# A streaming encoder layer on one core: one pass per tile with its own history length, and the modulation's products in four column groups

## The chip, the core and the metric

The kernel runs on one core of a Trainium2 chip. The metric is the device time of one execution in microseconds: 3823.52 as the median of three runs (3816.02 to 3826.64). The profile is of one further execution. Engines are named as the profile does: PE is TensorE (PEld its weight loads), DVE is VectorE, ACT is ScalarE, POOL is GpSimd, SP is SyncE, which issues most transfers.

## What is computed

One layer is applied to 64 new positions of a sample sequence (with 512 cached keys) and to a prompt of 1024 positions:

```
mod = silu(c) @ w_ada + b_ada            # c: (1024,), w_ada: (1024, 6144)
sh1, sc1, g1, sh2, sc2, g2 = split(mod, 6)
h   = rms_norm(x)*(1+sc1) + sh1
x   = x + g1 * (concat[SSD(h), FoX(h), ChunkMLP(h)] @ w_out)
x   = x + g2 * PEER(rms_norm(x)*(1+sc2) + sh2)
```

SSD is a chunked state-space scan, FoX is causal attention with a forget gate (4 heads of 64, blocks of 128 queries over all earlier keys), ChunkMLP mixes positions inside chunks of 128. PEER picks 128 experts for each position by product keys and sums their rows. All is float32. There are two vectors c, one of the prompt and one of the sample, so the modulation is a product of a 2 x 1024 matrix with w_ada.

## The kernel before

The program has two blocks; a barrier stands between them. The first (lines 167 to 816) does the modulation, the set-up and all token mixers, and writes x after the first sub-layer to the tensor `xmid` in memory. The second (lines 849 to 1226) does PEER: GpSimd gathers rows of the expert tables (line 913) into a ring of eight slots, VectorE forms dot products, ScalarE the weights, TensorE the weighted sums. The change does not touch the second block.

**The modulation** (lines 280 to 288 on TensorE). w_ada comes in 12 slices of 512 columns (2 MB each) through two buffers, which later hold w_out. SyncE issues slice c once the products of slice c-2 have ended (lines 182 to 199); the small inputs are issued between the first two slices and the others. For each slice, eight products (k = 0 to 7) with the two columns `silc[:, k, :]` as the stationary operand give a row of two partitions and 512 columns in PSUM. ScalarE copies the row to SBUF (line 498), and four transposes turn it into columns (line 277); the turn of slice c-1 stands behind the products of slice c. VectorE then adds the bias and makes the gains (line 609 on).

**The set-up** turns the first tile of x, spreads the gates over 128 rows (lines 303 to 305) and brings the 512 cached keys into the transposed form `kh` (lines 308 to 320). Then the first projection waits for W_in (line 328).

**The tiles.** Tile 0 holds the 64 sample positions, tiles 1 to 8 the prompt's eight blocks of 128. Each engine has its own function `tile`, which lists that engine's work for one tile in a fixed order; semaphores tie the engines together. On TensorE: projections (lines 332 to 344), the scan's and the keys' turns, the scores against the tile's own keys (line 380) and against the history (line 391, blocks of 512 keys into two banks in turn, each reduced to its maximum by VectorE in line 737 before the bank is used again), the scan's products (lines 398 to 400, which wait for the masked matrix of VectorE's line 727), the scores once more with keys on partitions (`by_key`, lines 418 to 422), ScalarE's exponentials of them (lines 558, 560), the weighing of the values (`weigh`, lines 429, 430), the ChunkMLP, the output projection (line 457). ScalarE keeps the tile's keys and values for later tiles (lines 580, 581). SyncE stores the middle result in line 222 when VectorE has ended line 797.

How many key tiles of history a tile computes is the argument HT:

```
tile(0, NPAST)                      # NPAST = 4
with pe.Fori(0, SHORT) as t:        # SHORT = 4
    tile(t + 1, SHORT)
with pe.Fori(SHORT, NT - 1) as t:   # LONG = NT = 8
    tile(t + 1, LONG)
tile(NT, LONG, last=True)
```

So tiles 0 to 4 compute four key tiles of history and tiles 5 to 8 eight, in blocks of 512 keys, although tile n of the prompt has n-1. Keys that are not there yet are hidden by a large negative number in row 64 of `kh` (line 808). Loops run on hardware registers, one on each engine. The semaphores `hist_scores`, `hist_max`, `key_scores` and `pT_exp` count in steps that give 8, 8, 24 and 24 in each tile, whatever HT is.

Of the kernel before, what the change touches and what calls it, by code (L numbers as in the profile page):

```python
# [7 lines left out]
ALU = mybir.AluOpType  # L8
# [65 lines left out]
def build(nc, a, o):  # L74


    with ExitStack() as ctx:
# [20 lines left out]
        silc = sb("silc", [P, KD, 2])  # L98
# [17 lines left out]
        with PA:  # L116
# [11 lines left out]
            hT = sa("hT", [P, KD, P])  # L128
            xbc = sa("xbc", [P, NB, P + 3])
# [5 lines left out]
            mod_row = (xtok[0:2, 0:512], um[0:2, :])  # L135
# [36 lines left out]
            SHORT, LONG = NPAST, NT  # L172
            assert SHORT < NT - 1

            @block.sync
            def _(sp):
                sp.dma_start(silc[:, :, :], a["c"]).then_inc(sem("c_in"), 16)
                sp.dma_start(xn[0:TS, :], a["x_sample"]).then_inc(sem("x_in"), 16)

# [52 lines left out]
                with sp.Fori(0, NT - 1) as t:  # L232
                    rows = bass.ds(t * P, P)
                    stores(t + 1, P, o["kp"][rows, :], o["vp"][rows, :], o["fp"][rows, :], xmid[rows, :], a["x_prompt"][rows, :], a["x_prompt"][bass.ds(t * P + P, P), :])
                rows = slice(SEQ - P, SEQ)
                stores(NT, P, o["kp"][rows, :], o["vp"][rows, :], o["fp"][rows, :], xmid[rows, :], a["x_prompt"][rows, :], None)
# [10 lines left out]
            def _(pool):  # L247
                for tile, value in ((ident, 0.0), (ones, 1.0), (upto, 1.0), (after, 1.0), (maskq, 0.0)):
                    pool.memset(tile[:, :], value).then_inc(pchain, 1)
# [9 lines left out]
                pool.memset(kh[:, :, :], 0.0).then_inc(sem("kh_clear"), 1)  # L259
# [10 lines left out]
            def _(pe):  # L270

                def mod_turned(c):
                    if c == 0:
                        pe.wait_ge(s_const, 1)
# [47 lines left out]
                def tile(n, HT, last=False):  # L322
                    T = T_OF(n)
# [14 lines left out]
                    prev(pe, sem("pT_exp"), n * 24)  # L338
# [37 lines left out]
                    if not FIRST(n):  # L376
                        pe.wait_ge(sem("hist_kept"), n)
                        pe.wait_ge(sem("hist_reset"), 1)
# [28 lines left out]

                    HB = HT // 4

                    def by_key(h):  # L410
                        for c in range(HB + 1):
                            i = h * (HB + 1) + c
                            bk = 5 + (c + 1) % 3 if HB == 2 else (5, 6)[c == 0]
                            if h:
                                pe.wait_ge(sem("pT_exp"), n * 24 + (i - HB) * (24 // (4 * (HB + 1))))
                            if c < HB:
                                for j in range(4):
# [5 lines left out]
                            mm.then_inc(sem("key_scores"), 24 // (4 * (HB + 1)))  # L423
# [845 lines left out]
```

## Time and profile before

| | |
|---|---|
| median of three runs | 3823.52 us |
| the profiled execution | 3826.0 us |
| its span (first to last instruction) | 3824.3 us |
| mean granted TensorE clock | 0.969 of full speed |
| busy in the span: PE, DVE, ACT, POOL | 3222.8, 2177.3, 1127.0, 1419.6 us |
| instructions | 30879 |

The span runs from the first instruction to the last; times inside it count from its start. A busy PE is not PE at its peak, since products overlap. An engine's idle time costs nothing unless the end waits for it, so the stages and the waits say more than the shares. A float32 product shows as two MATMUL instructions.

### The profile page before, as it was taken

How to read it: one execution, taken by the hardware profiler on the slowest of the kernel's cores; microseconds unless marked ns; L12 is line 12 of the kernel's file. 1: busy time of each engine (PE TensorE's matmuls, PEld its weight loads, DVE VectorE, ACT ScalarE, POOL GpSimd, SP SyncE). 2: the span in 40 equal slices, each digit the busy share in tenths (PEclk: the TensorE clock that was granted, in tenths of full speed). 3: DMA queues.
4: the chain of work that ended last, by engine and by line, in shares of the span. 5: the costliest groups of instructions: out<-in, count | busy, mean ns of one | idle time of the engine just before them, and what ended most of it. 6: DMA issues, size and time to landing. Idle time of an engine off the chain costs nothing.

```text
span 3824.3 us, 30879 instructions
## 1 busy us (share of the span) xinstructions
PE 3222.8 (84%) x9335; PEld 1496.6 (39%) x9335; DVE 2177.3 (57%) x5135; ACT 1127.0 (29%) x3428; POOL 1419.6 (37%) x1112
## 2 busy tenths in 40 slices
PE   8899999998888897798788779778878877987777
PEld 1566666665522333233233233323323323332222
DVE  0243333333468577568558757855865775685444
ACT  1123322222432323322332332232233233223222
POOL 0000000000044555455555555445555554555554
PEclk9789899999899999999999999999999999999999
DMA  8400000003099999999999999999999999999998
GB/s 270 180 19 19 19 19 20 21 29 114 24 405 378 422 421 421 420 422 419 417 418 417 418 417 419 415 418 420 416 417 419 418 414 413 422 419 419 419 417 356
DMA packets 195499, 1218.87 MB, mean 319 GB/s; under 512 B 34784, under 2 KB 35744, under 8 KB 54816
## 3 DMA queue, kind: packets, MB, share of 16 engines
q0 software_dynamic: 156672, 1140.92, 72.3%
q1 hardware_dynamic: 38688, 76.34, 5.7%
q8 instruction: 57, 0.93, 0.1%
q14 instruction: 82, 0.67, 0.0%
HBM read 1205.68 MB, written 11.50 MB: 318 GB/s over the span
## 4 chain that ended last, share of the span: by engine, by line
DMA 43%; PE 10%; issue 7%; DVE 6%; ACT 5%; POOL 4%; POOLq 0%; PEldq 0%
DMA shared<-in_uv,eidx_even 22%; DMA shared<-in_uv,eidx_odd 21%; PE bank L950 8%; DVE shared L1200 5%; POOL shared L913 4%; ACT wt L1028 2%; ACT dg L1032 1%; PE bank L938 1%; ACT ge L1025 1%; PE bank L961 1%; PE bank L921 0%; DVE ti L1089 0%; DVE shared L1091 0%; DVE shared L1124 0%; ACT dg L1052 0%
## 5 line engine op out<-in xcount | busy, mean ns | idle before, releaser
L950 PE MATMUL bank<-shared,dg 128*128 128x512 f32 (+1 forms) x4352 | 2032.1, 611 | 514.3 <-ACT dg L1032 514.2
L950 PEld LDWEIGHTS bank<-shared,dg 128*128 128x128 f32 (+1 forms) x4352 | 777.2, 188 | 1761.9 <-ACT dg L1032 927.1
L913 POOL DMA_INDIRECT shared<-in_uv,eidx_even x576 | 741.1, 1287 | 813.7 <-PE bank L950 627.9
L1200 DVE CUSTOM_DVE_ANT_0 shared<-shared,h_even 128x1024 f32<-128x1024 f32 x576 | 702.5, 1223 | 512.6 <-DMA shared<-in_uv,eidx_even 511.8
L913 POOL DMA_INDIRECT shared<-in_uv,eidx_odd x512 | 669.3, 1307 | 624.5 <-PE bank L950 547.7
L1200 DVE CUSTOM_DVE_ANT_0 shared<-shared,h_odd 128x1024 f32<-128x1024 f32 x512 | 625.4, 1222 | 422.2 <-DMA shared<-in_uv,eidx_odd 421.0
L1025 ACT ACTIVATE ge<-dots 128x2 f32<-128x2 f32 x544 | 110.6, 203 | 1866.3 <-DVE dots L1200 1866.2
L1032 ACT ACTIVATE dg<-ident,wt 128x128 f32<-128x128 f32 x1024 | 355.3, 394 | 16.7
L905 POOL IOTA iota<- 128x16 f32 x1 | 0.1, 145 | 942.2 <-POOLq L116 942.2
L938 PE MATMUL bank<-wk,h2T 128*128 128x512 f32 x576 | 288.5, 595 | 0.0
L343 PE MATMUL bank<-shared,hT 128*128 128x512 f32 (+3 forms) x576 | 221.2, 545 | 0.0
L938 PEld LDWEIGHTS bank<-wk,h2T 128*128 128x128 f32 x576 | 108.0, 190 | 141.6 <-issue 141.6
L343 PEld LDWEIGHTS bank<-shared,hT 128*128 128x128 f32 (+1 forms) x576 | 106.2, 186 | 108.5 <-issue 103.1
L1028 ACT ACTIVATE wt<-ge,gk_even 128x1 f32<-128x1 f32 x576 | 138.3, 287 | 9.4
L457 PE MATMUL bank<-wout,pT 128*128 128x512 f32 (+1 forms) x288 | 131.1, 614 | 0.0
L1028 ACT ACTIVATE wt<-ge,gk_odd 128x1 f32<-128x1 f32 x512 | 122.9, 287 | 8.4
L334 PEld LDWEIGHTS bank<-hT,shared 128*128 128x128 f32 x864 | 107.5, 208 | 4.2 <-issue 4.2
L334 PE MATMUL bank<-hT,shared 128*128 128x128 f32 (+1 forms) x864 | 107.7, 291 | 0.0
L284 PE MATMUL bank<-wout,silc 128*2 128x512 f32 x192 | 87.4, 610 | 15.9 <-DMA wout<-in_w_ada 15.9
L1200 DVE DVE_READ_ACCUMULATOR2_ANT dots<- 128x1 f32 x1088 | 89.9, 83 | 0.0
L795 DVE TENSOR_TENSOR mix<-bank,g1row 128x512 f32<-128x512 f32 (+1 forms) x18 | 11.6, 685 | 126.4 <-PE bank L457 126.4
L457 PEld LDWEIGHTS bank<-wout,pT 128*128 128x128 f32 (+1 forms) x288 | 55.2, 195 | 70.1 <-issue 70.0
(272 smaller groups left out, 2186.2 us busy)
## 6 DMA issues: line engine op xcount, KB each, us to landing
wout<-in_w_ada SPq DMA_DIRECT2D x12, 2048.0 KB, 8.2
shared<-in_w_in SPq DMA_DIRECT2D x1, 10288.0 KB, 33.6
shared<-in_uv,eidx_even POOLq DMA_INDIRECT x576, 12.5
shared<-in_uv,eidx_odd POOLq DMA_INDIRECT x512, 12.5
wout<-in_w_out SPq DMA_DIRECT2D x1, 4096.0 KB, 28.7
xn<-in_x_prompt SPq DMA_DIRECT2D x8, 512.0 KB, 4.8
xt<-in_x_prompt SPq DMA_DIRECT2D x8, 512.0 KB, 4.2
xmid<-mix SPq DMA_DIRECT2D x8, 512.0 KB, 2.9
```

The costliest lines, as they stand in the source:

```text
L284: mm = pe.matmul(bank[c % 2][0:2, :], silc[:, k, :], wada[:, c % 2, k, :], start=(k == 0), stop=(k == KD - 1))
L334: mm = pe.matmul(bank[2 + b // 4][:, (b % 4) * P:(b % 4) * P + T], win[:, k, b * P:(b + 1) * P], hT[:, k, 0:T], start=(k == 0), stop=(k == ...
L343: mm = pe.matmul(bank[bk][0:T, 0:w], hT[:, k, 0:T], win[:, k, col:col + w], start=(k == 0), stop=(k == KD - 1))
L457: mm = pe.matmul(bank[4 + c][0:T, :], mixT[:, k, 0:T], wout[:, k, 512 * c:512 * c + 512], start=(k == 0), stop=(k == KD - 1))
L913: pool.indirect_dma_start(ring[:, k % RING, :], None, a["uv"], bass.IndirectOffsetOnAxis(flat(eidxs[n % 2][:, :, :])[:, k:k + 1], 0)).then ...
L938: mm = pe.matmul(bank[S_BANK(n, c)][:, :], h2T[:, k, 0:P], wk[:, k, 512 * q:512 * q + 512], start=(k == 0), stop=(k == KD - 1))
L950: mm = pe.matmul(bank[SUM_BANK(n) + c][0:T, :], dg[:, k % RING, 0:T], ring[:, k % RING, DM + 512 * c:DM + 512 * c + 512], start=(k == 0), ...
L961: mm = pe.matmul(bank[b + k // 4][:, (k % 4) * P:(k % 4 + 1) * P], wqT[:, i, k * P:(k + 1) * P], cand[:, i * PK:(i + 1) * PK], start=True, ...
L1025: own.mark(act.activation(ge[:, ks[0]:ks[-1] + 1], dots[:, ks[0]:ks[-1] + 1], ACT.Gelu_apprx_tanh))
L1028: ins = act.activation(wt[:, k:k + 1], ge[:, k:k + 1], ACT.Copy, scale=gates[:, k:k + 1])
L1032: act.activation(dg[:, k % RING, 0:T], token[:, 0:T], ACT.Copy, scale=wt[:, k:k + 1]).then_inc(sem("dg"), 1)
L1200: ins = dve.tensor_tensor_reduce(ring[:, sl, 0:DM], ring[:, sl, 0:DM], h2s[n % 2][:, :], 1.0, 0.0, ALU.mult, ALU.add, dots[:, k:k + 1])
```

## The change

1. The history length is a function of the tile, `HIST(n)`: 4 for the sample, n-1 for prompt tile n. The number of 512-key blocks is `HB(n)`, the last of them only as wide as the history. All four engine programs run over n = 0 to 8 as straight code in place of loops. Semaphores count ones, and `HIST_BEFORE`, `KEYS_BEFORE` give what earlier tiles have counted. The clearing of `kh` by GpSimd and the large negative row by VectorE are gone. With no history at all (tile 1) the four heads' own scores go to banks 5, 6, 7 and 5 in turn.
2. In the modulation, product k uses array columns 32 (k mod 4) to 32 (k mod 4) + 31 and writes those PSUM partitions, so products k and k+4 add up in one group. The stationary operand has 32 columns, of which 30 are zero; it lies in the buffer `hT`, which GpSimd clears first, and the load of c waits for that and stands behind the load of x. ScalarE copies all 128 partitions. In place of four transposes, four products with a 128 x 2 selector (ones at rows 0, 32, 64, 96 and 1, 33, 65, 97) add the four groups and turn the row.

The core of the diff:

```diff
-        silc = sb("silc", [P, KD, 2])
+        sel = sb("sel", [P, 2])
...
+            silc = hT[:, :, 0:32]
...
-            mod_row = (xtok[0:2, 0:512], um[0:2, :])
+            mod_row = (xtok[:, 0:512], um[:, :])
...
-            SHORT, LONG = NPAST, NT
+            HIST = lambda n: n - 1 if n else NPAST
+            HB = lambda n: (HIST(n) + 3) // 4
+            HIST_BEFORE = lambda n: sum(FH * HB(m) for m in range(n))
+            KEYS_BEFORE = lambda n: sum(FH * (HB(m) + 1) for m in range(n))
+            KEY_BANK = lambda n, h, c: 5 + h % 3 if HB(n) == 0 else 6 - c if HB(n) == 1 else 5 + (c + 1) % 3
...
-                sp.dma_start(silc[:, :, :], a["c"]).then_inc(sem("c_in"), 16)
                 sp.dma_start(xn[0:TS, :], a["x_sample"]).then_inc(sem("x_in"), 16)
+                sp.wait_ge(sem("silc_clear"), 1)
+                sp.dma_start(silc[:, :, 0:2], a["c"]).then_inc(sem("c_in"), 16)
...
+                pool.memset(silc[:, :, :], 0.0).then_inc(sem("silc_clear"), 1)
...
-                pool.memset(kh[:, :, :], 0.0).then_inc(sem("kh_clear"), 1)
...
-                        mm = pe.transpose(bank[2][:, 2 * (4 * c + b):2 * (4 * c + b) + 2], mod_row[c % 2][:, b * P:(b + 1) * P], ident[0:2, 0:2])
+                        mm = pe.matmul(bank[2][:, 2 * (4 * c + b):2 * (4 * c + b) + 2], mod_row[c % 2][:, b * P:(b + 1) * P], sel[:, :], start=True, stop=True)
...
-                        mm = pe.matmul(bank[c % 2][0:2, :], silc[:, k, :], wada[:, c % 2, k, :], start=(k == 0), stop=(k == KD - 1))
+                        j = slice(32 * (k % 4), 32 * (k % 4) + 32)
+                        mm = pe.matmul(bank[c % 2][j, :], silc[:, k, :], wada[:, c % 2, k, :], start=(k < 4), stop=(k >= 4), tile_position=(0, 32 * (k % 4)))
...
-                        for c in range(HT // 4):
-                            i = h * (HT // 4) + c
+                        for c in range(HB(n)):
+                            i = h * HB(n) + c
+                            w = min(512, HT * P - 512 * c)
                             if i >= 2:
-                                pe.wait_ge(sem("hist_max"), n * 8 + (i - 1) * (8 // (4 * (HT // 4))))
-                            pe.matmul(bank[6 + i % 2][0:T, :], qT[0:AUG, h, 0:T], kh[0:AUG, h, 512 * c:512 * c + 512], start=True, stop=True)\
-                                .then_inc(sem("hist_scores"), 8 // HT)
+                                pe.wait_ge(sem("hist_max"), HIST_BEFORE(n) + i - 1)
+                            pe.matmul(bank[6 + i % 2][0:T, 0:w], qT[0:AUG, h, 0:T], kh[0:AUG, h, 512 * c:512 * c + w], start=True, stop=True)\
+                                .then_inc(sem("hist_scores"), 1)
...
-                                for j in range(4):
+                                for j in range(min(4, HT - 4 * c)):
...
-                tile(0, NPAST)
-                with pe.Fori(0, SHORT) as t:
-                    tile(t + 1, SHORT)
-                with pe.Fori(SHORT, NT - 1) as t:
-                    tile(t + 1, LONG)
-                tile(NT, LONG, last=True)
+                for n in range(NT + 1):
+                    tile(n)
...
-                    act.activation(mod_row[c % 2], bank[c % 2][0:2, :], ACT.Copy).then_inc(sem("mod_row"), 1)
+                    act.activation(mod_row[c % 2], bank[c % 2][:, :], ACT.Copy).then_inc(sem("mod_row"), 1)
...
-                                ins = act.activation((pT, pT2)[h % 2][:, 4 * c:4 * c + 4, 0:T], bank[bk][:, :].rearrange("p (j n) -> p j n", j=4)[:, :, 0:T], ACT.Exp)
+                                w = min(4, HT - 4 * c)
+                                ins = act.activation((pT, pT2)[h % 2][:, 4 * c:4 * c + w, 0:T], bank[bk][:, :].rearrange("p (j n) -> p j n", j=4)[:, 0:w, 0:T], ACT.Exp)
...
+                dve.wait_ge(s_const, 1)
+                then(dve.tensor_tensor(sel[:, :], ident[:, 0:2], ident[:, 32:34], ALU.add))
+                then(dve.tensor_tensor(sel[:, :], sel[:, :], ident[:, 64:66], ALU.add))
+                dve.tensor_tensor(sel[:, :], sel[:, :], ident[:, 96:98], ALU.add).then_inc(sem("sel"), 1)
...
-                            dve.tensor_reduce(mh[0:T, h, c + 1:c + 2], bank[6 + i % 2][0:T, :], X, ALU.max).then_inc(sem("hist_max"), inc)
+                            dve.tensor_reduce(mh[0:T, h, c + 1:c + 2], bank[6 + i % 2][0:T, 0:w], X, ALU.max).then_inc(sem("hist_max"), 1)
...
-                dve.memset(kh[64:65, :, :], GONE).then_inc(sem("hist_reset"), 1)
```

The loops of SyncE, ScalarE and VectorE go as TensorE's does.

## Rows read from the trace of the kernel before

**Rows 1.** The page, part 4: the chain that ended last, by line.
```profile
DMA 43%; PE 10%; issue 7%; DVE 6%; ACT 5%; POOL 4%; POOLq 0%; PEldq 0%
```

**Rows 2.** Busy times by stage: stretch, length, engines, then TensorE clock, DMA share, GB/s.
```profile
0.00:110.00 110.00, 91.28 (x240) 19.57 (x240) 0.19 (x1) 13.82 (x22) 8.97 (x23) 0.98 0.83 290
110.00:136.50 26.50, 17.62 (x73) 15.16 (x74) 13.37 (x46) 3.08 (x7) 0.00 (x0) 0.55 1.01 404
...
856.00:944.00 88.00, 82.81 (x417) 54.95 (x416) 33.62 (x82) 25.11 (x47) 0.00 (x0) 1.00 0.31 123
...
952.00:3824.00 2872.00, 2342.36 (x5352) 941.55 (x5352) 1857.17 (x4327) 876.31 (x2934) 1410.62 (x1089) 0.98 0.97 401
```

**Rows 3.** Timeline of SyncE, stores of the middle result: start, duration, line, operation.
```profile
237.49 0.48 SPq L222 DMA_DIRECT2D xmid<-mix  x1
...
323.03 0.35 SPq L222 DMA_DIRECT2D xmid<-mix  x1
...
408.37 0.36 SPq L222 DMA_DIRECT2D xmid<-mix  x1
...
671.35 0.36 SPq L222 DMA_DIRECT2D xmid<-mix  x1
...
763.66 0.36 SPq L222 DMA_DIRECT2D xmid<-mix  x1
```

**Rows 4.** Timeline of the score part: tile 3 (446 to 452), tile 6 (710 to 719).
```profile
446.68 1.29 DVE L727 TENSOR_TENSOR E<-E,cbm 128x512 f32<-128x512 f32 x2
...
447.41 1.88 PE L391 MATMUL bank<-kh,qT 97*128 97x512 f32 x4
...
451.41 1.90 PE L398 MATMUL bank<-xdt,E 128*128 128x64 f32 x16
...
710.40 1.88 PE L391 MATMUL bank<-kh,qT 97*128 97x512 f32 x4
...
715.52 0.69 DVE L737 TENSOR_REDUCE mh<-bank 128x1 f32<-128x512 f32 x1 [0.36 <-PE bank L391]
...
717.43 0.69 DVE L737 TENSOR_REDUCE mh<-bank 128x1 f32<-128x512 f32 x1 [0.36 <-PE bank L391]
718.09 1.90 PE L398 MATMUL bank<-xdt,E 128*128 128x64 f32 x16
```

**Rows 5.** The modulation: product groups, SyncE's wait, loads to landing, 30 to 40 us.
```profile
29.91 8.73 PE L284 MATMUL bank<-wout,silc 128*2 128x512 f32 x16 [1.30 <-DMA wout<-in_w_ada]
...
101.58 7.03 PE L284 MATMUL bank<-wout,silc 128*2 128x512 f32 x16 [1.62 <-DMA wout<-in_w_ada]
...
SPq L183 <- PE bank L284: 67.1, 9, 12.2
...
wout<-in_w_ada SPq DMA_DIRECT2D x12, 2048.0 KB, 8.2
...
30.00:40.00 10.00, 10.00 (x23) 1.93 (x22) 0.00 (x0) 0.59 (x1) 0.00 (x0) 0.83 0.52 182
```

**Rows 6.** Timeline of line 362: up to 443.30, then up to 443.70.
```profile
443.25 0.38 PE L362 MATMUL bank<-xc 64*128 64x128 f32 x2
...
443.25 0.49 PE L362 MATMUL bank<-xc 64*128 64x128 f32 x4
443.67 0.35 PE L290 MATMUL bank<-ident,ka 128*97 128x128 f32 x1
```

**Rows 7.** Last turn of the modulation, three issues of SyncE, W_in to landing.
```profile
109.29 0.41 PE L277 MATMUL bank<-ident,um 2*128 2x2 f32 x4 [0.34 <-ACT um L498]
...
0.82 0.38 SPq L177 DMA_DIRECT2D silc<-in_c  x1
...
14.57 1.22 SPq L191 DMA_DIRECT2D xbc<-in_conv  x1
...
92.77 0.58 SPq L200 DMA_DIRECT2D shared<-in_w_in  x1
...
shared<-in_w_in SPq DMA_DIRECT2D x1, 10288.0 KB, 33.6
```

More of the change, by code:

```diff
@@ L231, in _ @@
                 sp.dma_start(o["conv_s"], xbc[:, :, 0:3]).then_inc(sem("state_stored"), 16)
[L232 to L236, printed above, removed]
+                for t in range(NT):
+                    rows = slice(t * P, t * P + P)
+                    stores(t + 1, P, o["kp"][rows, :], o["vp"][rows, :], o["fp"][rows, :], xmid[rows, :], a["x_prompt"][rows, :], a["x_prompt"][t * P + P:t * P + 2 * P, :] if t < NT - 1 else None)
                 sp.wait_ge(sem("state"), NT + 1)
@@ L320, in _, with tile @@
                     mm.then_inc(sem("past_turned"), 1)
-                def tile(n, HT, last=False):
-                    T = T_OF(n)
+                def tile(n):
+                    T, HT, last = T_OF(n), HIST(n), n == NT
                     pe.wait_ge(sem("hT_dve"), n + 1)
@@ L406, in tile @@
                     pe.wait_ge(sem("qT"), 2 * n + 2)
-                    HB = HT // 4
                     def by_key(h):
[L411 to L416, printed above, removed]
-                                for j in range(4):
+                        for c in range(HB(n) + 1):
+                            i = h * (HB(n) + 1) + c
+                            bk = KEY_BANK(n, h, c)
+                            if h and HB(n):
+                                pe.wait_ge(sem("pT_exp"), KEYS_BEFORE(n) + i - HB(n))
+                            elif h == 3:
+                                pe.wait_ge(sem("pT_exp"), KEYS_BEFORE(n) + 1)
+                            if c < HB(n):
+                                for j in range(min(4, HT - 4 * c)):
                                     mm = pe.matmul(bank[bk][:, j * P:j * P + T], kh[0:AUG, h, (4 * c + j) * P:(4 * c + j + 1) * P], qT[0:AUG, h, 0:T],
@@ L429, in weigh @@
                             pe.matmul(bank[2][0:T, h * 65:h * 65 + 65], probs[:, j, 0:T], vh[:, j, h, :], start=(j == 0), stop=False)
-                        pe.matmul(bank[2][0:T, h * 65:h * 65 + 65], own[0:T, 0:T], vt[0:T, h, :], start=False, stop=True).then_inc(sem("pv"), 1)
+                        pe.matmul(bank[2][0:T, h * 65:h * 65 + 65], own[0:T, 0:T], vt[0:T, h, :], start=(HT == 0), stop=True).then_inc(sem("pv"), 1)
                     by_key(0)
@@ L502, in _, with tile @@
                     act.wait_ge(sem("past_turned"), j + 1)
[L503 to L504 removed]
                     act.activation(kh[0:AUG, :, j * P:(j + 1) * P], bank[6][0:AUG, :].rearrange("p (h n) -> p h n", h=FH), ACT.Copy).then_inc(sem("past_kept"), 1)
[L507 to L508 removed]
+                def tile(n):
+                    T, HT, last = T_OF(n), HIST(n), n == NT
                     act.wait_ge(sem("xbc_mm"), n + 1)
@@ L588, in tile @@
                         x_gained(n + 1)
-                start = then.n
-                tile(0, NPAST, None)
-                per = then.n - start
-                for tiles, HT in (((0, SHORT), SHORT), ((SHORT, NT - 1), LONG)):
-                    with act.Fori(*tiles) as t:
-                        then.loop(t, per, start + per)
-                        tile(t + 1, HT, t)
-                then.base, then.n = 0, start + per * NT
-                tile(NT, LONG, NT - 1, last=True)
+                for n in range(NT + 1):
+                    tile(n)
             @block.vector
@@ L653, in _, with tile @@
                     dve.wait_ge(sem("past_sum_used"), j + 1)
-                first = then.n
-                def tile(n, HT, last=False):
-                    T = T_OF(n)
+                def tile(n):
+                    T, HT, last = T_OF(n), HIST(n), n == NT
                     smp = FIRST(n)
@@ L797, in tile @@
                     dve.tensor_tensor(mix[0:T, :], mix[0:T, :], xt[0:T, :], ALU.add).then_inc(sem("xmid_ready"), 1)
-                tile(0, NPAST)
-                per = then.n - first
+                tile(0)
                 dve.wait_ge(sem("state_stored"), 48)
@@ L805, in _ @@
                 dve.memset(xbc[:, :, 0:3], 0.0)
-                dve.memset(fcar[:, :], 0.0)
-                dve.wait_ge(sem("pT_exp"), 24)
-                dve.memset(kh[64:65, :, :], GONE).then_inc(sem("hist_reset"), 1)
-                dve.wait_ge(sem("hist_reset"), 1)
-                start = then.n
-                for tiles, HT in (((0, SHORT), SHORT), ((SHORT, NT - 1), LONG)):
-                    with dve.Fori(*tiles) as t:
-                        then.loop(t, per, start)
-                        tile(t + 1, HT)
-                then.base, then.n = 0, start + per * (NT - 1)
-                tile(NT, LONG, last=True)
+                then(dve.memset(fcar[:, :], 0.0))
+                for n in range(1, NT + 1):
+                    tile(n)
         with ExitStack() as PB:
```

48 lines of the change are left out of this document (20 added, 28 removed).

## The prediction

> **What bounds the kernel now.** The page comes first: the span is 3824.3 us, and the chain that ended last is 43% gathers of the expert tables [rows 1]. The table of stages then splits the span: the modulation takes 110 us, the set-up 26.5 us, the tiles of the first block run to about 944, and from 952 on comes a second block of 2872 us in which the DMA engines are busy at a share of 0.97 [rows 2]. The change leaves that second block alone, so what it is worth comes from the first 952 us, and every microsecond saved there starts the second block earlier. Two stages of the first block are touched.
>
> In the tiles, the distance from one store of the middle result to the next is the time of a tile: 85.3 us where four key tiles of history are computed, 92.3 us where eight are [rows 3]. Four such short gaps and three such long ones stand there; the last tile, without a successor to prepare, takes 88.0 [rows 2]. So four more key tiles (times four heads) cost 7.0 us. That is the plain measure of the first half of the change.
>
> In the modulation, the product groups of slices 2 and 11 start at 29.9 and 101.6 us, so a slice takes 71.7/9 = 7.96 us [rows 5]. Each slice is 16 instructions of about 0.43 us (a float32 product is two), 7.03 us in all. Two buffers hold the slices, and the next load into a buffer waits for the products that read it: SyncE waited 67.1 us for TensorE on nine of them. A load takes 8.2 us to land, so a pair of slices costs 7.03 + 8.2 + 0.7 of hand-over = 15.9 us. Products and load stand in one chain, and neither engine is full: the DMA share up to 110 us is 0.83 [rows 2].
>
> **Part 1: each tile has its own number of key tiles.** Tile 0 (the sample) keeps 4. The prompt tiles had 4, 4, 4, 4, 8, 8, 8, 8 and get 0 to 7: 20 key tiles fewer. By the plain measure that is 20 x 7.0/4 = 35 us. The price is not even, though. The score part of a short tile, from the first history product to the products of line 398, takes 4.00 us, that of a long one 7.69: the first block of 512 keys costs 4.00, the second 3.69, which leaves 3.3 for exponentials and weighing [rows 4].
> - Tile 1 loses its first block whole. Line 398 must still wait for the mask products on VectorE, which end at 446.68 + 1.29 = 447.97, so 3.4 of the 4.00 go. Of the rest I take 5.5, because with the block also go its exponential and the wait for it in each head (bounds: 3.3, as in the second block, and twice that). About 9.
> - Tiles 2 to 4 lose 3, 2 and 1 of four, and TensorE's width, VectorE's width and the exponential all shrink: 6 x 9/4 = 13.5.
> - Tile 5 goes from two blocks to one: 7.0.
> - Tiles 6 to 8 lose 3, 2 and 1 of the second block. There the score loop keeps its pace by the wide blocks: reductions of the same bank start 1.91 us apart (715.52, 717.43), product, reduction and two hand-overs, whatever the narrow block beside it costs. So only the 3.3 per block goes and a little at the end: 6 x (0.83 + 0.23) = 6.4.
>
> The sum is 36 us. Its low end is 14: if a block cost the same however narrow, only the two blocks that vanish (tiles 1 and 5, 7.0 each) would count. Its high end is 42, with 11 for tile 1 and the full rate for tiles 6 to 8.
>
> The loops become straight code. The first pass of a loop, whose instructions are new to the engines, took 323.03 - 237.49 = 85.54 against 85.34 for the next pass [rows 3]. Five more tiles than before are run for the first time: 0 to +1 us, I take +0.5. What else goes with the loops (the clearing of the key history by GpSimd at the start and by VectorE in tile 1) lies beside the modulation's loads and beside tile 1's input projection, and counts nothing; were that cover gone, tile 1's convolution would start earlier and still wait for the same products. SyncE's stores keep their order.
>
> **Part 2: four column groups.** The 16 instructions of a slice go to four groups of 32 columns. If four ran at a time, a slice would take 4 x 0.43 = 1.7 us at 2.4 GHz, 3.4 at 1.2. If only neighbours of different groups overlapped (the two instructions of one product stay in one group), 9 x 0.43 = 3.9. If nothing overlapped, 7.03. The only work of the trace on separate parts of the array is line 362, two row groups: two of its four instructions start within 0.05 us of 443.25, but the next operation comes 0.42 us later, no sooner than four in a row [rows 6]. So starts are shared, a gain in time is not shown. I take 3.6 us, near the middle cases and above the best one, also because the clock does not stay at its upper level here: 0.83 in the mean from 30 to 40 us, after the wait for slice 2, and 0.55 in the set-up [rows 2, 5].
>
> The Trainium skill ("TensorE: Matmul & The Clock Gate", Part 3) gives 2.38 times for three column tiles of 512 columns, which would make 7.03/2.38 = 3.0 us here, an estimate by that page; the sum would be 3 us lower with it.
>
> With 3.6 us a pair takes 3.6 + 8.9 = 12.5, a slice 6.3: 9 x 1.66 = 15.0 us. The transfers stop this next: 110 us at a share of 0.83 hold 19 us of idle DMA, so no more than that can come out of the stretch. The last slice's products end the stage, -3.4. What is added:
> - The transposes become products with a selector over 128 rows, eight instructions for four. Four take 0.41 us, the last of them from 109.29 on [rows 7]; the last group is on the path, +0.4 at the upper clock and up to +1.2 at the lower; I take 0.7. The other eleven lie beside the loads.
> - The load of the vector c waits for GpSimd's clearing, stands behind the load of x and goes out in 1024 runs of 8 bytes. The nearest row, 768 runs of 12 bytes, took SyncE 1.22 us against 0.38 now [rows 7]. All of SyncE's loads behind it move by that: +0.8 (0.4 to 1.5). VectorE's three additions for the selector fall where it has nothing to do, and ScalarE's copies have as many columns as before, beside the loads.
>
> The load of W_in is issued behind the last slice's, at 92.77, and lands 33.6 us later, at 126.4, 10 us ahead of the first projection at 136.5 [rows 2, 7]. It moves forward with the last slice's load, the set-up with the last slice's products; the lead shrinks by the 3.4 us that those save, to some 7, and costs nothing.
>
> Part 2: -15.0 - 3.4 + 0.7 + 0.8 = -17 us. Ends: -24 (19 + 5 of the last slice) and +5 (rival 1).
>
> **Sum.** The profiled execution took 3826.0 us (its span and 1.7 around it): -36 + 0.5 - 17 = -52.5 gives 3773.5. The median of the runs is 2.5 lower, so the forecast for it is **3771 us**, its own range 3757 (-42 and -24) to 3785 (-30 and -9).
>
> **Rivals.**
> 1. **The column groups do not overlap in time** (or drop to the lower clock and take as long). For it: line 362's 0.42 us. Against: that row's instructions are short, and their fixed parts could hide a gain. Then TensorE paces a slice at 7.03 plus hand-over plus a longer turn, about 0.5 us more than now: +5 in 12 slices. -36 + 5 = -31: 3792 us. The Trainium skill ("TensorEngine Tiling", Key Properties) says that a change of tiling mode drains the engine; a slice would change twice, which works for this rival; no run here shows its price.
> 2. **History costs by blocks of 512, not by key tiles.** For it: the score loop's pace of 1.91 us. Against: products, reductions and exponentials are all cut to width. -14 - 17 = -31: 3792 us. Rivals 1 and 2 together: -9, 3814 us, which is no change.
> 3. **Slower: the gathers.** The buffer c has 64 bytes a partition, the selector that takes its place 8; every later buffer, the gathers' ring among them, may move by 56 bytes. If rows then land less well aligned, the second block pays: 1% of 2872 us is 29 us, and from 1.8% on this eats the 52.5; at 3% it would be -52.5 + 86, 3857 us. Nothing in the profile speaks for it, since all gathers have one alignment there; nothing excludes it.
>
> **Chances.** Forecast 0.76, rival 1 0.11, rival 2 0.07, both 0.03, rival 3 0.03. A measurement of this kernel can tell about 0.3%, 11.5 us, from no change. Faster by more: 0.76 + 0.11 + 0.07 = 0.94; within: 0.03; slower: 0.03. The range takes in the forecast's own and rivals 1 and 2 with a little for their ends: 3757 to 3796.
>
> **What would show it.** Right: middle-result stores about 76, 81, 82, 84, 85, 88.5, 89.5 and 87 us apart for tiles 1 to 8; first products of a slice 6 to 6.6 us apart; the last turn of the modulation over near 93 us instead of 109.7; the second block still 2872 us. Gaps of 85 in tiles 2 to 4 speak for rival 2. Slices still 8 us apart with TensorE busy throughout speak for rival 1; slices 5.8 apart with the DMA share near 1 would put the transfers in charge and the time at the low end. A second block longer by over 50 us is rival 3, and a tile 2 or 3 that takes longer than tile 1 by more than 10 us, with idle time before each first instruction, would mean that code fetches were underpriced. A time above 3800 makes the forecast wrong.

## The result, and the profile after

The changed kernel takes **3759.3 us** (median of 4 runs, 3758.65 to 3761.27) beside 3823.5 for the kernel before: a ratio of 0.9835, 95% interval 0.9822 to 0.9848, 64 us less. The forecast was 3771 with a range of 3757 to 3796, so time and sign are right, and the gain came out 12 us larger than worked out. The profiled execution has a span of 3756.9 us, 67.4 less than before; the sums below are made against that.

The chain of the page reads as before [rows 1]: gathers, which the change does not touch.

```profile
DMA 43%; PE 11%; issue 7%; DVE 6%; ACT 5%; POOL 4%; POOLq 0%; PEldq 0%
```

The windows by stage and, between the stores of the middle result (line 230), by tile. Behind the stretch and its length stand the busy time and instructions of PE, PEld, DVE, ACT and POOL; the last three columns are granted TensorE clock, DMA share and GB/s:

```profile
0.00:86.10 86.10, 54.23 (x288) 22.35 (x288) 0.48 (x3) 13.94 (x22) 5.77 (x23) 0.74 0.96 340
30.00:82.00 52.00, 41.54 (x216) 17.00 (x216) 0.00 (x0) 5.38 (x9) 0.00 (x0) 0.65 0.97 358
...
86.09:113.23 27.14, 17.97 (x73) 15.42 (x73) 13.55 (x46) 3.08 (x7) 0.00 (x0) 0.52 1.01 424
...
113.23:214.80 101.57, 100.00 (x400) 61.06 (x400) 29.96 (x83) 22.31 (x49) 0.00 (x0) 0.74 0.07 22
...
214.80:291.00 76.20, 68.56 (x309) 45.31 (x309) 30.93 (x82) 23.68 (x47) 0.00 (x0) 0.93 0.10 24
291.00:369.39 78.39, 71.34 (x331) 48.09 (x331) 31.27 (x83) 24.73 (x51) 0.00 (x0) 0.93 0.08 24
369.39:448.78 79.39, 73.15 (x347) 49.88 (x347) 31.80 (x83) 25.16 (x51) 0.00 (x0) 0.96 0.08 24
448.78:530.48 81.70, 76.22 (x363) 52.09 (x363) 32.30 (x83) 25.45 (x51) 0.00 (x0) 0.96 0.08 23
530.48:615.05 84.57, 79.80 (x379) 54.48 (x379) 32.93 (x83) 25.68 (x51) 0.00 (x0) 0.94 0.07 22
615.05:701.36 86.31, 80.54 (x403) 55.34 (x403) 33.74 (x87) 26.40 (x55) 0.00 (x0) 0.98 0.07 22
701.36:790.46 89.10, 84.54 (x419) 58.85 (x419) 34.26 (x87) 27.11 (x55) 0.00 (x0) 0.96 0.07 21
790.46:876.62 86.16, 80.39 (x401) 53.39 (x400) 32.91 (x82) 23.95 (x45) 0.00 (x0) 1.00 0.32 125
...
884.00:3756.90 2872.90, 2351.00 (x5352) 946.99 (x5352) 1856.33 (x4327) 876.25 (x2934) 1400.12 (x1089) 0.98 0.97 401
```

Four things are to be seen, beside [rows 2, 3]. The modulation ends at 86.1 instead of 109.7. The set-up behind it, up to the first projection at 113.2, takes 27.1 us (before 26.8, from 109.70 to 136.46). The second block, from 884 on, takes 2872.9 us (before 2872), at the same share and rate, and from the last store to the end it is 2880.3 us in the changed kernel and 2880.2 before: the gathers (rival 3) paid nothing. And each tile but the last has a mean granted clock below 1, between 0.93 and 0.98, a column that the prediction had read for the modulation and the set-up only.

TensorE's timeline of the changed kernel: products (line 291) and turns (line 283) of the modulation, of slices 2 and 11, then the wait ahead of the last head in tile 2.

```profile
30.27 3.64 PE L291 MATMUL bank<-wout,hT 128*32 128x512 f32 x16 [0.35 <-DMA wout<-in_w_ada]
33.84 1.87 PE L283 MATMUL bank<-sel,um 128*128 128x2 f32 x8
35.64 1.08 PE L291 MATMUL bank<-wout,hT 128*32 128x512 f32 x4
...
82.29 1.93 PE L291 MATMUL bank<-wout,hT 128*32 128x512 f32 x16 [0.67 <-DMA wout<-in_w_ada]
84.14 1.05 PE L283 MATMUL bank<-sel,xtok 128*128 128x2 f32 x8
85.06 1.03 PE L283 MATMUL bank<-sel,um 128*128 128x2 f32 x8
...
346.25 0.69 PE L436 MATMUL bank<-vh,E 128*128 128x65 f32 x2 [4.66 <-ACT pown L560]
```

A slice's 16 instructions take 1.93 us at the upper clock and 3.64 at the lower; slices are (82.29 - 30.27)/9 = 5.78 us apart, against 7.96. The first product after a turn starts 0.07 us before the end that the profile gives the turn (35.64 against 33.84 + 1.87). In the kernel before, which has no groups, a turn starts 0.08 us before the end of the products ahead of it, so no price of changing from four groups to the whole array shows. The Trainium skill ("TensorEngine Tiling (Array Packing)", Key Properties) has the engine drained at such a change. These rows, whose ends are modelled, show no time lost by it and cannot say more.

By the stores, the middle results come 22.7 us earlier at tile 0 (214.80 for 237.49), and tiles 1 to 8 save 44.8 together; 22.7 + 44.8 = 67.5 is the whole gain. Per tile (before minus after, from the stores; the clock columns are the lengths of the stretch at 0.50 in each tile, from windows of 0.2 us; the last column is explained below):

| tile | forecast | saved | at 0.50, before | at 0.50, after | saved with the clock held, no loops |
|---|---|---|---|---|---|
| 1 | 9 | 9.3 | 10.2 | 10.2 | 7.5 |
| 2 | 6.75 | 6.9 | 10.2 | 10.2 | 5.3 |
| 3 | 4.5 | 5.9 | 10.2 | 6.8 | 4.0 |
| 4 | 2.25 | 3.6 | 10.2 | 6.8 | 2.1 |
| 5 | 7.0 | 7.7 | 6.8 | 10.2 | 8.5 |
| 6 | 3.2 | 6.0 | 6.8 | 3.4 | 4.3 |
| 7 | 2.1 | 3.2 | 6.8 | 6.8 | 3.1 |
| 8 | 1.06 | 1.9 | 0 | 0 | 1.9 |
| sum | 36 | 44.8 | | | 36.8 |

Tile 5 gave the first hint. It has four key tiles now, as tiles 1 to 4 had before, and took 84.57 us against their 85.3, with 10.2 us at 0.50 in both. The first theory was that waits on constants, in straight code, hand over faster than those of a hardware loop.

### The profile page after: what moved, and what is told of

Same layout as the page of the kernel before. It is cut to its first block, busy times and chain, and to the rows that moved or that the text cites. A ratio compares the mean times of both kernels' runs of the same rounds, so it can differ in the third digit from the quotient of the medians.

```text
span 3756.9 us, 29484 instructions
## 1 busy us (share of the span) xinstructions
PE 3137.7 (84%) x9047; PEld 1463.3 (39%) x9047; DVE 2160.4 (58%) x5129; ACT 1117.8 (30%) x3418; POOL 1405.9 (37%) x1112
## 4 chain that ended last, share of the span: by engine, by line
DMA 43%; PE 11%; issue 7%; DVE 6%; ACT 5%; POOL 4%; POOLq 0%; PEldq 0%
DMA shared<-in_uv,eidx_even 22%; DMA shared<-in_uv,eidx_odd 21%; PE bank L936 8%; DVE shared L1186 5%; POOL shared L899 4%; ACT wt L1014 2%; ACT dg L1018 1%; PE bank L924 1%; ACT ge L1011 1%; PE bank L947 1%; PE bank L907 0%; ACT L984 0%; ACT L982 0%; DVE shared L1110 0%; DVE ti L1075 0%
## 5 line engine op out<-in xcount | busy, mean ns | idle before, releaser
L899 POOL DMA_INDIRECT shared<-in_uv,eidx_odd x512 | 660.5, 1290 | 633.8 <-PE bank L936 555.4
L1073 DVE MAX8 tv<-shared 128x8 f32<-128x128 f32 x272 | 59.1, 279 | 33.2 <-ACT shared L997 32.3
## 6 DMA issues: line engine op xcount, KB each, us to landing
shared<-in_uv,eidx_even POOLq DMA_INDIRECT x576, 12.5
shared<-in_uv,eidx_odd POOLq DMA_INDIRECT x512, 12.5
```

The source lines that it names most:

```text
L899: pool.indirect_dma_start(ring[:, k % RING, :], None, a["uv"], bass.IndirectOffsetOnAxis(flat(eidxs[n % 2][:, :, :])[:, k:k + 1], 0)).then ...
L1073: ins = dve.max(v[:, i, half], seg)
```

## The experiments

**Each half alone.** The two kernels take one half of the diff each: the first the modulation's lines (groups, selector, c in the buffer of hT), the second all the others. The line at the core of the first:

```diff
- mm = pe.matmul(bank[c % 2][0:2, :], silc[:, k, :], wada[:, c % 2, k, :], start=(k == 0), stop=(k == KD - 1))
+ mm = pe.matmul(bank[c % 2][j, :], silc[:, k, :], wada[:, c % 2, k, :], start=(k < 4), stop=(k >= 4), tile_position=(0, 32 * (k % 4)))
...
```

> The kernel before with the four column groups of the modulation alone; the tiles keep their loops and their 4 and 8 key tiles. Theory (four groups run at a time and the transfers set the pace): slices 5.8 us apart, products of a slice 1.9 us at the upper clock, the last turn of the modulation over at 86 us, all tiles as before; 23 to 24 us less, about 3800. The prediction's own step (products 3.6 us, load and products in one chain, 6.3 us a slice): the last turn at 93, 17 us less, about 3807. If the 23.6 us that the modulation gains were partly taken back by the set-up or the first tile, the first store of the middle result would stand later than 214.8 us.

> The changed kernel with the modulation as it was before (products on the whole array, transposes, c in a buffer of its own). Theory (39 us from key tiles left out, 5 from loops that are gone): tiles 1 to 8 as in the changed kernel within 0.5 us each (76.2, 78.4, 79.4, 81.7, 84.6, 86.3, 89.1, 86.2), 44 us less, about 3779. The prediction's own sum (36 less, 0.5 more): 3788. If the two parts help or hinder each other, the two savings of this run and of the modulation alone do not add up to the 64 to 67 us of the whole change.

The modulation alone: 3803.7 us (3797.8 to 3805.6), ratio 0.9944 (0.9929 to 0.9959), 20 less; its first store stands at 215.9, 21.6 earlier than before, and its tiles take 85.3 and 92.3 as before. The tiles alone: 3782.1 us (3779.5 to 3785.4), ratio 0.9893 (0.9877 to 0.9908), 42 less, with every tile within 0.3 us of the changed kernel's. 20 + 42 = 62 of 64: the halves hardly help or hinder each other. One miss: in the first kernel the last turn ends at 89.5 us and not at 86, with slices 6.10 us apart: its last two loads land 11.5 and 9.9 us behind their issue, 9.0 and 7.6 in the changed kernel. Its set-up makes up for part of that. Both times lie between the prediction's sum and the theory's.

**Straight code alone.** The tiles keep their padded numbers of key tiles, with the cleared and masked history.

```diff
- HIST = lambda n: n - 1 if n else NPAST
+ HIST = lambda n: NPAST if n < 5 else NT
```

> The kernel before with its loops unrolled and nothing else: every tile keeps its 4 or 8 key tiles, blocks of 512, and the masked, cleared key history; the modulation is as before. Theory (waits on constants hand over faster than the waits of a hardware loop): tiles 1 to 7 each 0.8 us shorter, 84.6 us for those with four key tiles and 91.5 for those with eight, 5 us less, about 3818. The prediction's own step (first runs of new code): 0 to 1 us more, tiles of 85.3 and 92.3 us. A third reading, that tile 5 of the changed kernel is shorter by its neighbours or its clock: tiles of 85.3 and 92.3, no change.

3811.4 us (10 runs, 3806.9 to 3817.1), ratio 0.9971 (0.9961 to 0.9980): 12 less, more than either theory allows. Tiles 3, 4 and 6 of it:

```profile
401.30:483.39 82.09, 77.32 (x379) 52.34 (x379) 32.95 (x83) 25.68 (x51) 0.00 (x0) 0.98 0.07 23
483.39:567.15 83.76, 78.98 (x379) 53.57 (x379) 32.95 (x83) 25.69 (x51) 0.00 (x0) 0.96 0.07 23
657.51:749.49 91.98, 89.64 (x451) 62.23 (x451) 35.72 (x87) 27.96 (x55) 0.00 (x0) 0.96 0.07 21
```

Tiles 3 and 4 are the same work, yet differ by 1.67 us, and tile 3 stands 3.2 below its like in the loops. What goes with it is the clock: 0.98 against 0.96, and 0.94 in the loops. So the waits of a loop cannot be the whole cause, since no code here loops. Before, tiles 2 and 6 ran at 0.50 for 10.2 and 6.8 us; the stretch begins in, or within 2 us behind, a wait of TensorE for the last head's exponential, which ScalarE computes behind the norms. The two stretches and the wait of tile 2 in the kernel before (the table above has the stretches of the changed one):

```profile
382.40:392.60 10.20, 8.97 (x36) 7.98 (x37) 4.48 (x11) 4.12 (x13) 0.00 (x0) 0.50 0.00 0
740.80:747.60 6.80, 6.80 (x31) 6.28 (x31) 2.73 (x8) 2.33 (x5) 0.00 (x0) 0.50 0.00 0
```

```profile
383.63 1.97 PE L429 MATMUL bank<-vh,E 128*128 128x65 f32 x8 [3.28 <-ACT pown L560]
```

A second theory, then: the same wait leads to a stretch at 0.50 that lasts 10.2, 6.8 or 3.4 us, and tiles that differ in that length differ in time by up to half of it.

**Is it groups that overlap, and what paces a slice now?** One group for all eight products, two groups, and four groups with a third buffer:

```diff
- j = slice(32 * (k % 4), 32 * (k % 4) + 32)
+ j = slice(0, 32)                              # one group
+ j = slice(32 * (k % 2), 32 * (k % 2) + 32)    # two groups
...
- wada[:, c % 2, k, :]
+ wada[c % 3][:, k, :]                          # wada[2] lies in kh; the load of slice c waits for the products of slice c-3
...
+ ada(2)                                        # issued ahead of the small inputs
```

> The changed kernel with all eight products of a slice in one and the same group of 32 array columns, one after the other; the turns work on 32 rows. It computes the same. Theory (the gain comes from groups that run at a time, not from weights of 32 columns instead of 2): nothing overlaps, a slice's 16 instructions take 7.0 us at the upper clock, slices 7.9 to 8 us apart, the last turn at 109 us, about 23 us more than the changed kernel. Rival (narrow weights or the form of the instruction make the products faster): products of a slice well under 7 us, last turn nearer 86.

> The changed kernel with the eight products in two column groups instead of four; the turns work on 64 rows. Theory (two groups run at a time, and the transfers set the pace so long as the products of one slice are shorter than the load of the other): products of a slice 3.5 to 3.7 us at the upper clock, slices 5.8 to 6.0 us apart, the last turn at 86 to 90 us. Rival (load and products of a buffer stand in one chain, as the prediction had it, half of landing plus products): 0.9 us more a slice, slices 6.6 us apart, the last turn near 95 us. By the prediction's number for four groups (3.6) this run would show what four groups were forecast to give.

> The changed kernel with a third buffer for the slices of the modulation, in the key history that nothing uses yet; three loads are under way at a time. Theory (the transfers already set the pace, DMA share 0.96 up to 86 us): each load takes longer to land, about 14 us instead of 8.8, slices 5.5 to 5.8 us apart, at most 3.4 us (the idle 4% of 86) less. Rival (landing and products of a buffer in one chain): slices come 3.6 to 4 us apart and the stage ends 15 us or more earlier, unless the load of the input projection's weights then ends last.

Products of a slice on TensorE, with one group and with two (one run each, 3782.0 and 3769.8 us):

```profile
29.60 7.05 PE L291 MATMUL bank<-wout,hT 128*32 128x512 f32 x16 [0.63 <-DMA wout<-in_w_ada]
...
101.83 7.05 PE L291 MATMUL bank<-wout,hT 128*32 128x512 f32 x16
```

```profile
29.78 6.13 PE L291 MATMUL bank<-wout,hT 128*32 128x512 f32 x16
36.81 3.63 PE L291 MATMUL bank<-wout,hT 128*32 128x512 f32 x16
...
85.50 5.32 PE L291 MATMUL bank<-wout,hT 128*32 128x512 f32 x16 [3.49 <-DMA wout<-in_w_ada]
91.74 3.63 PE L291 MATMUL bank<-wout,hT 128*32 128x512 f32 x16
```

With one group, 7.05 us: slices are (101.83 - 29.60)/9 = 8.03 us apart, about as before the change, and the last turn ends at 110.8. So 32 columns of weights bring nothing, and the groups bring it all: 7.05, 3.63 and 1.93 us at the upper clock for one, two and four. The Trainium skill ("TensorE: Matmul & The Clock Gate", Part 3) has 2.38 times for three column tiles of 512 columns. No run here has three; two and four gave 1.94 and 3.65 times, more for each group than that figure. With two groups slices came 6.88 us apart and the last turn ended at 97.2, where the theory of transfers in charge said 5.8 to 6.0 and 86 to 90, and the chain of load and products 6.6 and near 95. The third buffer, products and windows (slices; then tile 0), and loads to landing:

```profile
35.04 3.31 PE L293 MATMUL bank<-kh,hT 128*32 128x512 f32 x16
...
78.34 3.64 PE L293 MATMUL bank<-kh,hT 128*32 128x512 f32 x16
82.98 1.03 PE L285 MATMUL bank<-sel,um 128*128 128x2 f32 x8
```

```profile
30.00:74.00 44.00, 35.37 (x208) 16.55 (x212) 0.00 (x0) 8.34 (x14) 0.00 (x0) 0.69 1.03 396
...
110.57:206.62 96.05, 94.48 (x400) 58.65 (x400) 29.93 (x83) 22.29 (x49) 0.00 (x0) 0.79 0.05 12
```

```profile
wout<-in_w_ada SPq DMA_DIRECT2D x8, 2048.0 KB, 11.5
...
kh<-in_w_ada SPq DMA_DIRECT2D x4, 2048.0 KB, 12.8
```

Slices are (78.34 - 35.04)/9 = 4.81 us apart, at 396 GB/s. So the two-buffer kernel was not at the transfers' limit, though its DMA share from 30 to 82 us reads 0.97: it moved 358 GB/s. Neither forecast for the third buffer came out whole. The pace lies between the theory's (5.5 to 5.8) and the rival's (3.6 to 4), and the stage ends only 2.1 us earlier (84.0 for 86.1), which the theory had (at most 3.4) and the rival had not (15 or more). Two things in the trace stand behind this. Three loads under way have a pace of their own, since two slices in a row that both wait for their loads start 5.1 us apart:

```profile
67.84 2.93 PE L293 MATMUL bank<-wout,hT 128*32 128x512 f32 x16 [2.19 <-DMA wout<-in_w_ada]
...
72.97 3.64 PE L293 MATMUL bank<-wout,hT 128*32 128x512 f32 x16 [0.41 <-DMA wout<-in_w_ada]
```

And the third load stands ahead of the small inputs: ScalarE's first work behind those begins at 28.37 us instead of 23.18, so that the first turn and slice 2 start about 5 us later.

What paces the changed kernel is read from its own trace. SyncE's issue of slice 4, into the buffer of slice 2, and the products of slice 4:

```profile
33.97 0.37 SPq L191 DMA_DIRECT2D wout<-in_w_ada  x1
...
43.16 3.38 PE L291 MATMUL bank<-wout,hT 128*32 128x512 f32 x16 [2.86 <-DMA wout<-in_w_ada]
```

The products of slice 2 end at 30.27 + 3.64 = 33.91, the next load goes out 0.06 us later, and its products start 9.19 us behind that. Each of the four rounds of this buffer, from slice 2 to slice 10, is such a chain; they take 12.9, 11.1, 11.3 and 11.7 us, in the mean 3.3 for products, 8.4 from issue to the next products and 0.06 between. With two groups the rounds take 13.0 to 15.2, with products of 5.3 to 6.1. **So the prediction's chain of load and products stands for two buffers, and transfers alone do not set the pace there.** The one-group run is no test of it, since TensorE waits for a load in only two of ten slices (0.63 and 0.39 us); nor was the kernel before:

```profile
30.00:82.00 52.00, 50.00 (x131) 10.60 (x130) 0.00 (x0) 3.52 (x6) 0.00 (x0) 0.97 0.74 258
```

In all the kernel with the third buffer takes 3753.7 us (3748.3 to 3757.5), ratio to before 0.9819 (0.9801 to 0.9836), and its first store comes 8.2 us earlier. Of these 2.1 are the modulation's, 0.6 the set-up's and 5.5 tile 0's, 96.05 us at a granted clock of 0.79 against 101.57 at 0.74: half of the 12.4 us by which the time at 0.50 shrank (52.4 to 40.0, from windows of 2 us) is 6.2. Again the clock, in a stage that neither edit touched.

**The clock held.** Idle products fill the wait ahead of the last head; nothing reads what they write.

```diff
+ for _ in range(FILL[n]):    # 0, 12, 11, 10, 8, 7, 6, 5, 0 in the changed kernel; 8 and 3 in the others
+     pe.matmul(bank[2][:, 260:512], ident[:, :], win[:, 0, 0:252], start=True, stop=True)
  weigh(FH - 1)
```

> The changed kernel, with 12, 11, 10, 8, 7, 6 and 5 idle products (128x252, into the unused columns of bank 2, which nothing reads) in tiles 1 to 7 just ahead of the last head's weighing, where TensorE otherwise stands still for 1.9 to 4.7 us and from where its granted clock is 0.50 for 10.2, 10.2, 6.8, 6.8, 10.2, 3.4 and 6.8 us. Theory (what the sum of key tiles did not explain in tiles 2 to 7 is the length of these stretches, which differs between the two kernels): without them each tile gives back half of its stretch, tiles of about 71.1, 73.3, 76.0, 78.3, 79.5, 84.6, 85.7 and 86.2 us, 27 us less, about 3732. Rival (the excess came from waits on constants in straight code, the clock stretch being beside other work): tiles as they are, or longer by what the idle products overrun, 3759 to 3763.

> The kernel before, in its loops, with 8 (short tiles) and 3 (long tiles) of the same idle products at the same place; its stretches at 0.50 are 10.2 us long in tiles 1 to 4 and 6.8 us in tiles 5 to 7. Theory: 5.1 and 3.4 us less a tile, short tiles about 80.3, long ones 88.9, 30.6 us less, about 3793; long minus short is then 8.6 us and not 7.0, the plain price of four key tiles without the clock. That is also where the straight code's tiles come out when half of their stretches is taken off (80.3 to 80.4 and 88.6 to 88.7), so that loops as such cost nothing. Rival (loops hand over more slowly, by 0.8 us a tile): short tiles 81.1 or more, long ones 89.5 or more.

> The straight code alone (4 and 8 key tiles, modulation as before), with the same 8 and 3 idle products as the looped kernel of the run before last, so that the two differ in nothing but loops. Theory (loops as such cost nothing; the straight code's 14.5 us came from shorter stretches at 0.50): short tiles within 0.2 us of 81.43, long ones within 0.2 of 89.49, tile 8 88.1, in all within 3 us of that kernel's 3803. Rival (waits of a loop cost time at every hand-over): short tiles 80.7 or less, long ones 88.7 or less, 5 us or more below it.

The changed kernel with idle products: tiles 1, 2 and 5, and the wait of tile 1 on TensorE:

```profile
214.29:288.04 73.75, 70.79 (x333) 46.94 (x333) 30.86 (x82) 23.61 (x47) 0.00 (x0) 1.00 0.11 25
288.04:363.78 75.74, 73.01 (x353) 49.09 (x353) 31.21 (x83) 24.72 (x51) 0.00 (x0) 1.00 0.08 25
519.80:600.67 80.87, 78.90 (x393) 53.24 (x393) 32.86 (x83) 25.67 (x51) 0.00 (x0) 1.00 0.07 23
```

```profile
262.05 5.32 PE L446 MATMUL bank<-shared,ident 128*128 128x252 f32 x24
267.38 0.44 PE L439 MATMUL bank<-vt,pown 128*128 128x65 f32 x2
268.33 1.10 PE L451 MATMUL bank<-vn,wsT 128*128 128x64 f32 x8 [0.51 <-DVE vn L776]
```

The kernel before (tiles 2 and 6), then the straight code with padded tiles (the same two):

```profile
321.42:402.85 81.43, 79.18 (x395) 53.56 (x395) 32.85 (x83) 25.68 (x51) 0.00 (x0) 1.00 0.07 23
655.20:744.68 89.48, 87.68 (x457) 59.96 (x457) 35.63 (x87) 27.97 (x55) 0.00 (x0) 1.00 0.07 21
```

```profile
321.16:402.21 81.05, 79.08 (x395) 53.68 (x395) 32.87 (x83) 25.67 (x51) 0.00 (x0) 1.00 0.07 23
653.72:743.12 89.40, 87.66 (x457) 60.04 (x457) 35.64 (x87) 27.95 (x55) 0.00 (x0) 1.00 0.07 21
```

The clock is 1.00 in all of them. The changed kernel takes 3740.95 us (3739.3 to 3742.8), ratio to before 0.9780 (0.9764 to 0.9796); tiles 1 to 8 take 643.94 instead of 661.82. The rival is out, but the theory's 27 us were too many, since 17.9 came: half of a stretch is its price only where TensorE alone sets the pace. In tile 2 the stretch begins 3.1 us before the wait ends (343.1 against 346.25), and there it slows nothing; in tile 1 the 24 instructions of filler end at 267.4, and the next product still waits for VectorE. The one-group run has the same tiles 1 and 2 with 6.8 us at 0.50 in place of 10.2, and they are only 0.25 and 0.15 us shorter.

The kernel before gains 24.1 in its tiles and not 30.6 (706.61 to 682.50; 3803.0 us, 3797.4 to 3804.4). Its 81.43 and 89.48 us are what the rival of that run had named (81.1 or more, 89.5 or more), so the loops had still to be priced. A long tile costs 8.05 more than a short one and not 7.0.

Straight code without loops stands at 680.74 (3797.1 us, 3793.1 to 3802.9): 0.36 to 0.38 us less in a short tile, between the two expectations, and 0.08 to 0.10 in a long one, as the theory had it. The whole time lies 5.9 us lower, as the rival had it, but the runs of the two kernels overlap and the tiles account for 1.8. Even in the tiles the two kernels differ in more than loops, because the same idle products outlast the wait of the straight code by more. The last exponential and the products that need it, in tile 6 of the straight code:

```profile
720.82 0.27 ACT L564 ACTIVATE pown<-bank 128x128 f32<-128x128 f32 x1
...
721.50 0.67 PE L436 MATMUL bank<-vh,E 128*128 128x65 f32 x5
```

The exponential ends at 721.09, and the products start 0.41 us later; in the looped kernel 0.19 us, and 0.05 where the filler is no longer than the wait. In short tiles it is 0.33 against 0.06. If all of this is passed on, a loop costs 0.6 us in a short tile and 0.3 in a long one, 3.4 in seven tiles. Two other pairs speak for that. Tile 5 of the changed kernel, the same four key tiles with a filler that fits, takes 80.87 us against 81.43 in the loop. And tile 6, with 6.8 us at 0.50 in both, takes 92.31 in the kernel before and 91.98 in straight code. So a loop does cost something, 1.8 to 3.4 us in seven tiles, where the first theory had 5.

With these the 44.8 us of the tiles come apart, the second value with the filler's excess taken off. Work: 680.74 - 643.94 = 36.8 (the table's last column), or 34.8. Loops: 682.50 - 680.74 = 1.8, or 3.4. Clock: 24.1 - 17.9 = 6.2, or 6.6.

**Both, and the set-up.** The third buffer, the idle products in the tiles, and more of them in the set-up's waits:

```diff
+ def idle(k):
+     for _ in range(k):
+         pe.matmul(bank[7][:, 0:P], ones[:, :], ident[:, :], start=True, stop=True)
...
+ idle(8)
  pe.wait_ge(sem("setup_read"), 1)
```

> The changed kernel with the third buffer for the modulation, the idle products in tiles 1 to 7, and further idle products (128x128 into bank 7) in the waits of TensorE during the set-up, after which tile 0 runs its first 24 us at a granted clock of 0.50. Theory: 6 us less by the buffer, 27 by the tiles, and up to 12 by tile 0 (half of 24 us), less if the idle products delay the chain of the set-up: 3713 to 3726. If the idle products of the set-up do not raise the clock ahead of tile 0, no gain there and up to 3 us lost: 3726 to 3729.

**3724.5 us** (3722.9 to 3725.9), ratio 0.9737 (0.9721 to 0.9753): the fastest of all, 35 us below the changed kernel and within the 3713 to 3726 expected, though by smaller terms: 16.1 us came from the tiles, where 27 were expected, and 6.4 from tile 0, where up to 12 were. The windows from 81 us to the first projection, and of tile 0:

```profile
81.00:109.10 28.10, 25.02 (x141) 21.57 (x137) 13.57 (x46) 3.68 (x8) 0.00 (x0) 0.75 1.01 423
...
109.10:198.77 89.67, 88.10 (x401) 50.07 (x400) 29.93 (x83) 22.29 (x49) 0.00 (x0) 0.85 0.07 22
```

The clock of the set-up, 0.52 in the changed kernel, is 0.75 here, and tile 0 takes 89.67 us at 0.85 where the third buffer alone had 96.05 at 0.79. Its time at 0.50 fell from 40.0 to 27.3 us, and half of that is 6.3. It starts 1.5 us earlier too (109.10 for 110.57). The last tile lost 1.7 us (87.86 for 86.17): a wait of 1.1 us for VectorE was there followed by 3.4 us at 0.50, which the changed kernel does not show.

## Why the prediction was right, and where its sizes were off

**Tiles, 36 us.** The sum was right for the work (34.8 to 36.8), but in part by luck, since its terms were off in both directions. By the table's last column, in which up to 0.3 us a tile can be filler, tiles 1 to 4 were forecast at 22.5 and give 18.9; tile 1 is worth 7.5 and not 9. Tiles 5 to 8 were forecast at 13.4 and give 17.9. The reason is the "plain measure": 92.3 - 85.3 = 7.0 [rows 3] compares tiles with 6.8 and 10.2 us at the lower clock. With the clock held four key tiles cost some 8 us, and tile 5, which loses a whole block, saves 8.5. That narrow blocks beside wide ones bring little more than their 3.3 a block was too careful in tiles 6 (4.3 for 3.2), 7 (3.1 for 2.1) and 8 (1.9 for 1.06). Rival 2, by blocks of 512, needs 0 in tiles 2 to 4; they save 5.3, 4.0 and 2.1. The distances of the stores under "What would show it" do not come out of the prediction's sum: for tiles 2, 3, 4, 6 and 7 it gives 78.6, 80.8, 83.1, 89.1 and 90.2 us, and the list has 81, 82, 84, 88.5 and 89.5. Measured were 78.4, 79.4, 81.7, 86.3 and 89.1. The -30 and -9 behind its own upper bound stand there without working.

**Straight code, +0.5 us.** This step failed. It had priced code that is new to the engines from the first and second pass of a loop (85.54 against 85.34), and nothing else. Measured alone, straight code takes 12.5 us off the tiles (706.61 to 694.09): 1.8 to 3.4 by the loops that go, the other 9.1 to 10.7 by shorter stretches at the lower clock (37.6 us in the eight tiles for 61.5). In the changed kernel, whose stretches are 54.6 us long together, 6.2 to 6.6 us of clock and the loops are left. The prediction named no row of the tiles' clock.

**Modulation, -17 us against -23.6.** The steps stood, their sizes did not. Slices: 9 x (7.96 - 5.78) = 19.6 for 15.0. Last products: 7.03 - 1.93 = 5.1 for 3.4. Last turn: 1.03 - 0.41 = 0.6 for 0.7. The load of c cost 0.4 (slice 2 starts at 30.27 for 29.91) for 0.8. The 3.6 us for a slice's products was chosen as a middle between products that overlap in part and 1.7. Four groups do run at a time, and take 1.93 us at the upper clock and 3.64 at the lower. In the chain's rounds they took 3.3 in the mean, because the clock from 30 to 82 us is 0.65 (0.97 in the kernel before); so 3.6 was near for the slices, which is luck, and missed for the last one, which ran at the upper clock. In the pair of slices the larger miss is the hand-over: 8.2 + 3.6 + 0.7 = 12.5 was forecast, 8.4 + 3.3 + 0.06 = 11.7 measured. The 0.7 came from the kernel before, of which the prediction says that neither engine is full; TensorE was busy for 50.0 of 52 us there and waited for a load in six of ten slices only, so a landed slice often had to wait for TensorE. Slices came 5.78 us apart and the last turn ended at 86.1, earlier than the 6 to 6.6 and 93 that were to show the forecast right. Its sentence that slices 5.8 apart at a share near 1 would put the transfers in charge does not hold: at that distance and a share of 0.97, the third buffer still brought them to 4.8. Rival 1 is dead by the one-group run, which shows what it would have looked like.

**Set-up and W_in.** Costed at nothing, and 0.4 us longer than before (27.14 for 26.76). W_in goes out at 75.05 and lands 32.0 us later, 6.2 us ahead of the first projection; the prediction had some 7. Tile 0 came out 0.5 us longer (101.57 for 101.03), with 52.4 us at the lower clock for 51.4.

The sum: 23.6 - 0.9 + 44.8 = 67.5 against 52.5 forecast; 6.6 of the difference are the modulation's, 8.8 the tiles' (6.2 clock, 1.8 loops, 0.8 work; with the filler's excess taken off 6.6, 3.4 and -1.2), 0.5 the price set on straight code, and set-up and tile 0 take 0.9 back.

## What to carry to other kernels

Before a difference between two stretches is taken for the price of the work in them, compare their granted clock: here a plain 7.0 us were some 8 with the clock held, and 9 to 11 of the 12.5 us that unrolling alone took off the tiles were clock. A known wait of TensorE ahead of a long run of products is worth filling with idle products, if bank columns are free; compare their end with the end of the wait, since an overrun of 0.3 us blurred the price of the loops here. And a DMA share near 1 does not say that transfers pace a stage; the GB/s beside it, and one more buffer, say more.

## What the runs showed of the hardware

- Column groups: 16 float32 instructions of 128x512 (eight products) take 7.05, 3.63 and 1.93 us in one, two and four groups of 32 columns, at the upper clock.
- Tiles of straight code with the same four key tiles ran at a granted clock of 0.50 for 3.4, 6.8 or 10.2 us after the same wait. That idle products in the wait keep it at 1.00 is shown; why one tile got 3.4 and the next 6.8 stays open.
- A pass of a hardware loop over a tile cost 0.4 to 0.6 us more than the same straight code in short tiles (81.43 us against 81.06, and against 80.87 in tile 5 of the changed kernel), 0.1 to 0.3 in long ones (89.48 against 89.40; 92.31 against 91.98 with 6.8 us at 0.50 in both). But for that last pair the clock is 1.00 in all of them.
- Two 2 MB loads under way moved 358 GB/s at a DMA share of 0.97, three 396 at 1.03 (slices that wait for their loads start 5.1 us apart), and the load of W_in beside others 424 at 1.01.
